# Copying both halves of an operand in one instruction: ACT and DVE in the MLP of a float32-accurate encoder block

## What is computed

```python
def hybrid_layer(x, ...):
    ...
    x = x + y @ w_out
    u = rms_norm(x, norm_mlp_g) @ w_up          # 1024 -> 4096
    u = jnp.square(jax.nn.relu(u))
    return x + u @ w_down                       # 4096 -> 1024
```

## Time and profile before

| | |
|---|---|
| three runs | 1147.22, 1149.58, 1151.62 us; median 1149.58 |
| the profiled execution | 1149.14 us, of which the span of its instructions is 1147.4 us |
| granted TensorE clock, mean | 0.996 |
| PE busy | 1117.8 us, 97% of the span |
| DVE, ACT, POOL busy | 769.8 us (67%), 535.6 us (47%), 197.5 us (17%) |
| from the first down product to the end | 536 to 1147 us |

### The profile page before, as it was taken

One profiled execution on the slowest core, in us unless ns is written; L12 is line 12 of the kernel. 1 busy time (PEld: TensorE's weight loads), 2 busy tenths in 40 slices (PEclk: granted clock), 3 DMA queues, 4 the chain that ended last, 5 costly groups with the idle time before them and its releaser, 6 DMA issues.

```text
span 1147.4 us, 15385 instructions
## 1 busy us (share of the span) xinstructions
PE 1117.8 (97%) x5528; PEld 928.9 (81%) x5528; DVE 769.8 (67%) x1353; ACT 535.6 (47%) x1018; POOL 197.5 (17%) x202
## 2 busy tenths in 40 slices
PE   6999999999999999999999999999999999999995
PEld 5898888789999988888788778888888888888874
DVE  4625314477666556464977997949859769589497
ACT  5521213366576545264334345255264353452555
POOL 2430496121214000200100100001001001010025
PEclk9999999999999999999999999999999999999998
DMA  9522112575445442521210210221112112201204
GB/s 236 141 74 56 47 46 83 114 165 114 86 86 129 115 134 83 165 83 46 74 37 1 74 47 27 74 74 37 55 56 74 37 37 74 70 18 60 74 19 147
DMA packets 54235, 90.97 MB, mean 79 GB/s; under 512 B 5904, under 2 KB 23312, under 8 KB 54160
## 3 DMA queue, kind: packets, MB, share of 16 engines
q1 hardware_dynamic: 54160, 89.99, 28.5%
HBM read 68.97 MB, written 4.19 MB: 64 GB/s over the span
## 4 chain that ended last, share of the span: by engine, by line
PE 87%; DVE 7%; ACT 2%; issue 1%; DMA 1%; POOL 0%; POOLq 0%; SPq 0%; ACTq 0%; DVEq 0%
PE ps L1051 24%; PE ps L1053 24%; PE ps L1052 24%; PE ps L1259 5%; DVE xr L2017 2%; PE ps L1281 2%; PE ps L951 2%; PE ps L1217 1%; DVE w_lo L1862 1%; DVE uv_lo L1883 1%; PE ps L1232 1%; PE ps L1218 1%; PE ps L1201 1%; PE ps L1244 1%; DMA pj<-x_prompt 1%
## 5 line engine op out<-in xcount | busy, mean ns | idle before, releaser
L1051 PE MATMUL ps<-w_hi,uv_hi 128*128 128x512 f32 x448 | 177.1, 395 | 2.7 <-DVE w_lo L1862 1.4
L1051 PE MATMUL ps<-hT,w_hi 128*128 128x512 f32 x448 | 177.1, 395 | 0.0
L1053 PE MATMUL ps<-w_hi,uv_lo 128*128 128x512 f32 x448 | 176.8, 395 | 0.0
L1053 PE MATMUL ps<-hT,w_lo 128*128 128x512 f32 x448 | 176.8, 395 | 0.0
L1052 PE MATMUL ps<-hT,w_hi 128*128 128x512 f32 x448 | 176.7, 395 | 0.0
L1052 PE MATMUL ps<-w_lo,uv_hi 128*128 128x512 f32 x448 | 176.7, 394 | 0.0
L1001 DVE SCALAR_TENSOR_TENSOR w_lo<-w_raw,w_gain,w_hi 128x512 fp32r<-128x512 f32 (+1 forms) x88 | 70.6, 807 | 141.1 <-ACT w_hi L992 140.3
L2017 DVE TENSOR_TENSOR xr<-ps,xr 128x512 f32<-128x512 f32 x224 | 140.3, 677 | 6.6 <-PE ps L1053 6.2
L992 ACT ACTIVATE w_hi<-w_raw,w_gain 128x512 fp32r<-128x512 f32 (+1 forms) x88 | 61.4, 703 | 172.1 <-PE ps L1053 167.5
L1051 PE MATMUL ps<-w_hi,hT 128*128 128x512 f32 (+1 forms) x320 | 120.7, 377 | 0.0
L1053 PE MATMUL ps<-w_hi,hT 128*128 128x512 f32 (+1 forms) x320 | 119.3, 373 | 0.0
(11 more groups left out here) (159 smaller groups left out, 2012.0 us busy)
## 6 DMA issues: line engine op xcount, KB each, us to landing
w_raw<-w_in SPq DMA_DIRECT2D x48, 256.0 KB, 2.6
stk<-stg SPq DMA_DIRECT2D x32, 256.0 KB, 3.6
w_raw<-w_out SPq DMA_DIRECT2D x32, 256.0 KB, 2.6
raw<-w_down SPq DMA_DIRECT2D x32, 256.0 KB, 2.9
turn<-w_down SPq DMA_DIRECT2D x32, 256.0 KB, 2.9
w_raw<-w_up SPq DMA_DIRECT2D x24, 256.0 KB, 2.8
turn<-w_up SPq DMA_DIRECT2D x24, 256.0 KB, 2.9
raw<-w_up SPq DMA_DIRECT2D x24, 256.0 KB, 2.9
```

Source lines behind the costliest of these rows:

```text
L1051: nc.tensor.matmul(out, a_hi, b_hi, start=first, stop=False, skip_group_check=onto)
L1053: return nc.tensor.matmul(out, a_lo, b_hi, start=False, stop=last, skip_group_check=onto)
```

## The change

Where the two halves lie side by side, one instruction of 1024 columns takes the place of two of 512: on ACT for the `hi` of a weight pair, on DVE for the `lo` of a weight pair and for the `lo` of every u operand. A pair from `turn1` stays two instructions, as do the first pieces of chunks 0 and 1 that are issued one by one. ACT's `u_high` is not changed. The merged instruction waits for what both halves waited for, and counts its semaphore up by 2 at its end.

```diff
+        def pair_block(role, ph):
+
+            if role in ("11", "22"):
+                return (raw11 if role == "11" else raw22)[:, :, :]
+            n = ({"12": 0, "21": 1, "sum": 2}[role] - ph) % 3
+            return None if n == 1 else (turn0 if n == 0 else turn2)[:, :, :]
+
+        def weight_pair(c, up, v):
+            return pair_block(ROLES[v], phase_of(c, up))
...
+            def pair_high(n, c, up, v):
+
+
+                for kt in range(2):
+                    wait_weight(act, c, up, v, kt)
+                free_slot(act, n + 1)
+                s = n % W_SLOTS
+                nc.scalar.copy(w_hi[:, s:s + 2, :], weight_pair(c, up, v)).then_inc(hi_split, 2)
+
             def seven_high(c, v):
 
+                if weight_pair(c, True, v) is not None:
+                    pair_high(seven_piece(c, v, 0), c, True, v)
+                    return
...
+            def down_both_high(c, v):
+
+                if weight_pair(c, False, v) is not None:
+                    pair_high(down_piece(c, v, 0), c, False, v)
+                else:
+                    down_high(c, v, 0)
+                    down_high(c, v, 1)
...
             def chunk_down(c):
                 u_high(c, "S2")
-                down_high(c, 2, 0)
-                down_high(c, 2, 1)
+                down_both_high(c, 2)
...
+            def pair_low(n, c, up, v):
+
+                dve.wait_ge(hi_split, n + 2)
+                s = n % W_SLOTS
+                nc.vector.tensor_tensor(w_lo[:, s:s + 2, :], weight_pair(c, up, v), w_hi[:, s:s + 2, :].bitcast(F32),
+                                        ALU.subtract).then_inc(lo_split, 2)
...
             def u_low(c, name):
-                for kt in range(2):
-                    dve.wait_ge(uv_hi_ready, high_no(c, name, kt) + 1)
-                    nc.vector.tensor_tensor(uv_lo[:, u_slot(c, name), kt, :], u_source(name, kt),
-                                            uv_hi[:, u_slot(c, name), kt, :].bitcast(F32), ALU.subtract).then_inc(uv_lo_ready, 1)
+
+                dve.wait_ge(uv_hi_ready, high_no(c, name, 1) + 1)
+                blk = {"A11": 0, "S2": 0, "A12": 1, "S4": 1, "S1": 2, "S3": 2, "A22": 3}[name]
+                nc.vector.tensor_tensor(uv_lo[:, u_slot(c, name), :, :], sqf[:, blk, :, :],
+                                        uv_hi[:, u_slot(c, name), :, :].bitcast(F32), ALU.subtract).then_inc(uv_lo_ready, 2)
```

More of the change, by code:

```diff
@@ L1585, in last_down_high @@
                 u_high(c, "S4")
-                down_high(c, 5, 0)
-                down_high(c, 5, 1)
+                down_both_high(c, 5)
                 u_high(c, "S3")
-                down_high(c, 4, 0)
-                down_high(c, 4, 1)
+                down_both_high(c, 4)
                 u_high(c, "A22")
@@ L1594, in last_down_high @@
                 nc.scalar.activation(rms[:, 3, 0, 1:2], eps[:, 0:1], ACT.Sqrt)
-                down_high(c, 6, 0)
-                down_high(c, 6, 1)
+                down_both_high(c, 6)
                 for t in range(TPB):
@@ L1612, in chunk_up @@
                 h_high(3)
-                down_high(c, 0, 0)
-                down_high(c, 0, 1)
+                down_both_high(c, 0)
                 down_high(c, 1, 0)
@@ L1643, in chunk_seven @@
                 block_squares(c, 2)
-                down_high(c, 1, 0)
-                down_high(c, 1, 1)
+                down_both_high(c, 1)
             def chunk_down(c):
                 u_high(c, "S2")
-                down_high(c, 2, 0)
-                down_high(c, 2, 1)
+                down_both_high(c, 2)
                 u_high(c, "S1")
-                down_high(c, 3, 0)
-                down_high(c, 3, 1)
+                down_both_high(c, 3)
                 if c == NCHUNK - 1:
@@ L1661, in chunk_down @@
                 for v, name in ((4, "S4"), (5, "A22")):
-                    down_high(c, v, 0)
-                    down_high(c, v, 1)
+                    down_both_high(c, v)
                     u_high(c, name)
-                down_high(c, 6, 0)
-                down_high(c, 6, 1)
+                down_both_high(c, 6)
                 if c + 1 < SEVEN:
@@ L1863, in down_low, with down_both_low @@
                                         w_hi[:, n % W_SLOTS, :].bitcast(F32), ALU.subtract).then_inc(lo_split, 1)
+            def pair_low(n, c, up, v):
[3 more added lines that the diff above has]
+                                        ALU.subtract).then_inc(lo_split, 2)
+            def down_both_low(c, v):
+                if weight_pair(c, False, v) is not None:
+                    pair_low(down_piece(c, v, 0), c, False, v)
+                else:
+                    down_low(c, v, 0)
+                    down_low(c, v, 1)
             def seven_low(c, v):
+                if weight_pair(c, True, v) is not None:
+                    pair_low(seven_piece(c, v, 0), c, True, v)
+                    return
                 for kt in range(2):
@@ L2037, in last_down_low @@
                 u_low(c, "S4")
-                down_low(c, 5, 0)
-                down_low(c, 5, 1)
+                down_both_low(c, 5)
                 u_low(c, "S3")
                 add_x(c, 3)
-                down_low(c, 4, 0)
-                down_low(c, 4, 1)
+                down_both_low(c, 4)
                 u_low(c, "A22")
@@ L2047, in last_down_low @@
                 add_x(c, 5)
-                down_low(c, 6, 0)
-                down_low(c, 6, 1)
+                down_both_low(c, 6)
                 add_x(c, 4, (0,))
@@ L2084, in chunk_up @@
                 h_lows(2)
-                down_low(c, 0, 0)
-                down_low(c, 0, 1)
+                down_both_low(c, 0)
                 h_lows(3)
@@ L2133, in chunk_down @@
                 if c >= SEVEN:
-                    down_low(c, 1, 0)
-                    down_low(c, 1, 1)
+                    down_both_low(c, 1)
                 sum_s1(c, 0)
@@ L2140, in chunk_down @@
                 u_low(c, "S2")
-                down_low(c, 2, 0)
-                down_low(c, 2, 1)
+                down_both_low(c, 2)
                 add_x(c, 0)
@@ L2145, in chunk_down @@
                 sum_s3(c)
-                down_low(c, 3, 0)
-                down_low(c, 3, 1)
+                down_both_low(c, 3)
                 add_x(c, 1)
```

## The result

| | before | with the change |
|---|---|---|
| median of the runs (6 each) | 1149.31 us | 1156.86 us |
| lowest to highest | 1147.22 to 1151.62 | 1156.07 to 1157.94 |
| span of the profiled execution | 1147.4 | 1155.3 |
| granted TensorE clock, mean | 0.996 | 0.992 |

The ratio is 1.0063, 95% interval 1.0049 to 1.0076: slower by 7.5 us, more than what a measurement can tell from no change.

The account below looks back on a forecast made before the run. TensorE bounds the kernel, so only its waits count. Added waits at product 4, chunk 2's fifth up block and chunk 7's product 5 sum to 4.9 us, giving 1154.3 us, 0.41% more; range 1150 to 1158.

Parts of the forecast that it names:

- the class that was thought likeliest, no change: Whole kernel: measured time within about 0.5% (5.7 us) of before; chance 0.70, against 0.28 slower and 0.02 faster.
- PE bounds, and only its waits matter; the change can lose more than it can win: MLP: TensorE busy 1117.8 of 1147.4 us; at most 5.4 us of waits can be won, losses have no cap.
- The coarser hand-over at S2, A12, A11 and at awaited weight pairs: DVE waits for ACT's second half: free 0.38 us later per awaited weight pair, 0.55 at S2; added stalls sum to 4.9.
- The pair saves DVE 0.05 us: Each merged DVE subtraction: 1232 ns, engine free after 1.15 us against 1.21 for two singles; 7 us over 133 pairs.
- slower rival: The pairs behind the waits in each chunk: merging saves DVE nothing, 1.8 us more, 6.7 us in all, 1156.1; chance 0.26.
- Cover of 0.09 us at product 4: Down product 4, chunks 2 to 6: PE's held loader hides 0.09 us of delay, leaving stalls of 0.21 or 0.64.
- The clock, to which I gave almost nothing: Chunk 2's longer stall: rival that TensorE's clock falls there; given almost nothing, as the 2.8 us stall showed no lower clock.
- Relief alone, faster: At existing waits: ACT has both halves done when DVE comes, only the 0.05 us savings count; 1.0 us less, 1148.5; chance 0.09.
- The rule of the Trainium skill: ACT and DVE, 47% and 67% busy: unsaturated, so grouping puts this kernel on the wrong side; not in the sum.

Follow-up runs that it names:

- all pairs and three moves: The change with all its pairs, plus three DVE moves putting what PE waits for first (chunk 2, product 4, chunk 7): 1147.01 us, ratio 0.9975 to the kernel before.
- chosen pairs: The change with pairs only for down weights 3 to 6 and u operands S1, S3, S4, A22, all else by halves: 1149.31 us, ratio 0.9987 to before.
- kernels with reductions: The kernel before, no pairs, with one or two more DVE reductions at each of two places in chunks 2 and 7: 1152.50 and 1153.34 us, single executions.
- weights alone: The change with DVE's u operands by halves again, weight pairs kept: 1153.60 us, ratio 1.0025 to the kernel before.
- u operands alone: The kernel before with u operands merged on DVE as in the change, weights by halves: 1156.14 us, ratio 1.0051 to the kernel before.
- reordered, no pairs: The kernel before, without pairs, with three DVE moves putting what PE waits for first: 1145.85 us against 1150.23, ratio 0.9963.

## Why the prediction was right or wrong

The range held the 1156.86 us, but the class that was thought likeliest, no change, did not come; the kernel is slower, at the upper side of the range. That the range reaches there is in part luck: its upper end was put there for a merged instruction that saves nothing, whose 1156.1 us is close to the measured time, and the runs show another cause. Point by point:

- *PE bounds, and only its waits matter; the change can lose more than it can win.* Right. 15 us less work on DVE and ACT bought nothing.
- *The coarser hand-over at S2, A12, A11 and at awaited weight pairs.* Right in place and size: every stall forecast came, none came in an up block of chunks 3 to 7, and the sum of stalls was 5.2 us for 4.9. The run with pairs only where DVE comes late, and the one with all pairs and three moves, show both sides of it. In chunks 0 and 1 part of the stall came one product earlier, at product 3. I had compared the ends of `w_lo` alone; product 3 waits for the `xr` additions of product 1, which had next to nothing in hand. In the sum that changes nothing.
- *The pair saves DVE 0.05 us.* It saved 0.07, and the row of 1219 ns stands beside the 1232 worked out; the ACT copy is 1049 ns for 1050. The slower rival, that merging saves nothing on DVE, is wrong.
- *Cover of 0.09 us at product 4.* Too much. DVE idles 0.67 us more at S2 where I had 0.60, and starts 0.49 later at weight 1 (1.13 us after ACT's copy starts, 0.64 before) where I had 0.43. With 0.07 saved in each of six pairs that makes 0.25 us in chunk 2 and 0.74 in chunk 3; the stalls are 0.20 and 0.71. A loader that was already held had 0.03 to 0.05 us left. The small errors cancelled: each stall came out within 0.07 us.
- *The clock, to which I gave almost nothing.* This is the step that failed. I took full clock after a stall of 2.8 us as leave to have no term, though the change was to lengthen that very stall by 0.84 and chunk 7's by 0.7. It was 3.2 us in the profile, 1.6 at each place, and it turns a forecast of "same" into "slower": the stalls alone, 5.2 us, are under the 5.7 us of that line. The two kernels with longer stalls and no pair show that it needs no merged instruction and comes with the stall. The two medians differ by 7.5 us, less than the 5.2 + 3.2 us of the two profiles, very likely since the kernel before has falls in some executions.
- *Relief alone, faster.* Wrong for this change, for the reason given: ACT's second half is not there when DVE comes. For the kernel with the chosen pairs it is right in direction: 1.1 us, of which shorter stalls are 0.5.
- *The rule of the Trainium skill* (Perfetto Trace Analysis, Optimizing Scalar/DVE Operations) that breaking instructions up may end work sooner where these engines aren't saturated but make another wait: the runs agree. Undoing just the pairs that are waited for took the kernel from 7.5 us over before to 1.1 under.

## What to carry to other kernels

Merging two instructions lengthens the time to the first half; it pays only where the consumer comes after the whole is done anyway. So ask of each merged pair who waits for it, and how long PE's loader had been held there, not how busy the engine is. And when a change lengthens a stall of TensorE, put in a term for its clock: a run at full clock after a shorter stall is no proof for the longer one.

## What the runs showed of the hardware that was not expected

- TensorE's granted clock was at its half level (1.2 of 2.4 GHz) for 3.4 us around the restart after stalls of 3.71 and 2.14 us (the change), 3.54 and 1.99, 4.21 and 2.59 (the kernels with reductions), 3.21 (weights alone), 3.02 (chosen pairs), and 3.54 in chunk 2 with u operands alone; not after 2.94 and 1.40 (before), nor in chunk 7 after 2.27 (reordered, no pairs), 2.04 (weights alone), 1.92 (u alone) and 1.25 (chosen pairs). Length of the stall doesn't tell it alone: 1.99 had it, and 2.04 and 2.27 hadn't. It began between 0.2 us before PE's restart (687.40 for 687.62 in the change) and 1.1 us after it (689.13 for 687.99 with weights alone).
- Each fall cost PE 1.4 to 1.6 us in slow steps, whatever the stall's length.
- The first matmul after a stall steps 0.31 to 0.34 us to the next at full clock, in place of 0.23.
- DVE once took 2.38 us for two subtractions of 512 columns in place of 1.28, the second of them 1.78. POOL multiplied beside it, but it did so beside the 1.28 us of the kernel before too; the cause stays open.
